# One chunk of the u products per head moved from the retrieval stage into the gate stage

## The chip, the cores and the metric

The kernel runs on one core of one Trainium2 chip. The metric is the device time of one execution in microseconds (us); lower is better. The engines are TensorE (PE for matmuls, PEld for its weight loads), VectorE (DVE), ScalarE (ACT), GpSimd (POOL) and SyncE (SP), which only issues transfers here.

## The reference, cut to what matters

The kernel computes one decoder layer: normalisation, attention and recurrence branches, their merge, and then a retrieval over 16384 single-neuron experts. Only this last part, `peer_ffn`, is touched. For 512 tokens it is

```python
q = (x_c @ w_q).reshape(128, 8, 256)              # 8 heads
s1, s2 = q[..., :128] @ sub_k1.T, q[..., 128:] @ sub_k2.T
t1, i1 = lax.top_k(s1, 16); t2, i2 = lax.top_k(s2, 16)
top_s, pos = lax.top_k(t1[..., :, None] + t2[..., None, :], 16)   # of the 256 sums
ids = the 16 of i1 * 128 + i2 at pos
gate = softmax(top_s)
hid = gelu(einsum('chkd,cd->chk', u[ids], x_c))
out = einsum('chk,chkd->cd', gate * hid, v[ids])
```

## The kernel before

The kernel does not gather u and v for most tokens. For three of the four tiles of 128 tokens (384 tokens) it computes the products of the tokens with **all** 16384 rows of u, in 128 chunks of 128 rows, applies gelu and stores 128 x 384 numbers per chunk in `HID_scratch`. It builds a matrix G of gates (expert by token, zero where an expert is not picked), multiplies the two and forms the product with all of v. The fourth tile's tokens gather their own rows of u and v instead, one gather of 128 rows (512 KB) per head and pick.

**A chunk m of the u products** (`hidden_layer`) is this chain: `load` brings 512 KB of u into a slot (L1377); `split_hi` on ScalarE rounds it to a high part (L1387); `split_lo` on VectorE makes the low part (L1397); `product` on TensorE is 8 x 3 matmuls of 384 columns (L88 to L90); `gelu` on ScalarE (L1393); `store` writes 192 KB to `HID_scratch` (L1381). There are five slots while the retrieval runs and two afterwards, so `load(m)` waits for `split_lo` of the chunk that had the slot before: five chunks back, later two chunks back.

**`peer_retrieval`** runs eight heads. Each head is a long chain of small steps on VectorE: the top 16 of 2 x 4 score tiles (L1580 to L1584), the candidate sums and their top 16 (L1607 to L1611), an index search (L1617 to L1640) that ends in the list of picks `gidx` (L1640), the softmax (L1650 to L1652). Between these steps stand, in an order written out by hand, 16 dot products of rows gathered for the previous head (`dot`, L1565) and the chunks' `split_lo` (`lo(h, j)` is that of chunk h * UPH + j + 2). TensorE does UPH chunks per head, and in the first seven heads the two projections and the scores of the next head (`project`, `score`). ScalarE and SP run matching loops. UPH is 13 before, so the retrieval does NRC = 8 * 13 + 2 = 106 chunks.

**`gate_matrix`** builds G in 96 steps of four tokens. VectorE makes one-hot rows (L1760, L1765), TensorE multiplies them (L1789), ScalarE copies the result into `g_stage` (L1803). Every 32 steps a tile is complete and SP stores its 8 MB as eight transfers of 1 MB (L1738). Beside the steps, each group of four steps takes one chunk: TensorE does a quarter of it per step, VectorE its `split_lo` after the fourth step, ScalarE `split_hi`, `gelu` and the store. BESIDE = 15 chunks are done so, up to chunk TAIL = 121; the other seven (121 to 127) follow behind the steps. GpSimd's queue is, in this order:

```python
for m in range(NRC + GSLOT, TAIL + GSLOT + 1):
    load(pool, m)                       # waits for split_lo of chunk m - 2
pool.wait_ge(g_stored[1], 8 * 16)       # tile 1 of G has been stored
for j in range(TOPK):                   # 16 gathers of the last head's rows, into g_stage's second half
    nc.gpsimd.indirect_dma_start(...)
for m in range(TAIL + GSLOT + 1, NCHUNK):
    load(pool, m)
```

VectorE, behind its last step, does `split_lo(TAIL + 1)`, waits until all 16 gathers have landed, and then does 16 dot products (L1774) with one `split_lo` ahead of every third, chunks 123 to 127. The stage ends when all engines are done and all stores have landed; then `experts` starts with the loads at L1861.

Of the kernel before, what the change touches and what calls it, by code (L numbers as in the profile page):

```python
# [35 lines left out]
NQ = SEQ // P  # L36
# [33 lines left out]
PH = 8  # L70
NK = 128
TOPK = 16
NCHUNK = 128
ND = 3
TD = ND * P
UPH = 13
USLOT = 5
GSLOT = 2
NRC = PH * UPH + 2
NCAND = 88  # L80
# [1338 lines left out]
def peer_retrieval(nc, d, keep):  # L1419
# [6 lines left out]
    with ExitStack() as ctx:  # L1426
# [46 lines left out]
        @block.sync  # L1473
        def _(sp):
            for m in range(PH * UPH):
                h, j = m // UPH, m % UPH
                if j in (0, 1) and h < PH - 1:
                    sp.wait_ge(w_lo, h * 2 + j + 1)
                    sp.dma_start(wraw[:, j], d["w_q"][h * 2 + j + 2]).then_inc(w_in[j], 16)
                if m >= 1:  # L1480
                    load(sp, m + USLOT - 1)
                    store(sp, m - 1)
            for m in range(PH * UPH - 1, NRC):
                store(sp, m)

        @block.scalar
        def _(act):
# [26 lines left out]
            for h in range(PH):  # L1514
                for j in range(UPH):
                    m = h * UPH + j
                    if h < PH - 1:
# [31 lines left out]
        def _(dve):  # L1549
# [7 lines left out]
            def dot(h, k):  # L1557

                if h == 0:
                    return  # L1560
                j = (h - 1) * TOPK + k
                dve.wait_ge(row_in[j % GBUF_R], j // GBUF_R * 16 + 16)
                if j > 0:
                    dve.wait_ge(rows_eaten, j)
                nc.vector.tensor_tensor_reduce(dump[:], urows[:, j % GBUF_R], x2t[:], 1.0, 0.0, ALU.mult, ALU.add,  # L1565
                                               hdot[:, j:j + 1]).then_inc(rows_eaten, 1)

            def lo(h, j):

                split_lo(dve, h * UPH + j + 2)  # L1570
# [5 lines left out]
            for h in range(PH):  # L1576
# [29 lines left out]
                for i in range(NQ):  # L1606
                    link(nc.vector.max(ctop[:, i, 0:8], cand[:, i]))  # L1607
                    link(nc.vector.match_replace(crest[:, i], ctop[:, i, 0:8], cand[:, i], -3.0e38))
                    nc.vector.max_index(cpos[:, i, 0:8], ctop[:, i, 0:8], cand[:, i])
                    link(nc.vector.max(ctop[:, i, 8:16], crest[:, i]))  # L1610
                    link(nc.vector.max_index(cpos[:, i, 8:16], ctop[:, i, 8:16], crest[:, i]))  # L1611
                    dot(h, 2 * NQ + i)
                    if h == PH - 1:
                        lo(h, 2 * NQ + i)
                    elif i != 1:
                        lo(h, (7, None, 8, 9)[i])
                nc.vector.tensor_tensor(shifted[:], ctop[:], ctop[:, :, 0:1].broadcast_to([P, NQ, TOPK]),  # L1617
# [13 lines left out]
                    eq[:].rearrange("p j q k a -> p (j q k) a"),  # L1631
                    cabf[:].rearrange("p j q k -> p (j q k)").unsqueeze(2).broadcast_to([P, 2 * NQ * TOPK, TOPK]),
                    iota[:].unsqueeze(1).broadcast_to([P, 2 * NQ * TOPK, TOPK]), ALU.is_equal))
                lo(h, 12 if h == PH - 1 else 10)
                flat = eq[:].rearrange("p j q k a -> p (j q) k a")
                link(nc.vector.tensor_tensor(
                    flat, flat, idxf[:].rearrange("p j q a -> p (j q) a").unsqueeze(2).broadcast_to([P, 2 * NQ, TOPK, TOPK]),
# [6 lines left out]
                    lo(h, 11)  # L1644
                for k in range(3 * NQ, TOPK):
                    dot(h, k)
                    if k == TOPK - 2 and h < PH - 1:
                        lo(h, 12)
                dve.wait_ge(exp_done, h + 1)
                link(nc.vector.reduce_sum(gsum[:, 0], gates[:], AX.X))  # L1650
                link(nc.vector.reciprocal(gsum[:, 1], gsum[:, 0]))
# [46 lines left out]
def gate_matrix(nc, d, keep):  # L1698
# [6 lines left out]
    TB = 4  # L1705
    NS = P // TB
    STEPS = ND * NS
    BESIDE = 15
    TAIL = NRC + BESIDE
    QA = NK // 8  # L1710
    NBANK = 4
    LATE = (PH - 1) * TOPK
    with ExitStack() as ctx:
# [18 lines left out]
        @block.sync  # L1732
        def _(sp):
            for tile in range(ND):
                sp.wait_ge(staged, NS * (tile + 1))
                for r in range(8):
                    a = slice(r * QA, (r + 1) * QA)
                    sp.dma_start(G[a, :, tile * P:tile * P + P].rearrange("a b t -> b a t"),  # L1738
                                 stage[:, tile % 2, a]).then_inc(g_stored[tile % 2], 16)
            sp.wait_ge(g_stored[0], 2 * 8 * 16)  # L1740
# [14 lines left out]
        def _(dve):  # L1755
            for n in range(STEPS):
# [6 lines left out]
                for t in range(TB):  # L1763
                    t1 = slice(n * TB + t, n * TB + t + 1)
                    nc.vector.tensor_scalar(hot1[:, b, t], iota[:], picksT[:, 0, t1], picksT[:, 2, t1],  # L1765
                                            ALU.is_equal, ALU.mult).then_inc(hot1_made, 1)
                if n % 4 == 3 and n // 4 <= BESIDE:
                    split_lo(dve, NRC + n // 4)
# [10 lines left out]
        def _(pe):  # L1779
            for n in range(STEPS):  # L1780
                if 4 <= n < 4 + 4 * BESIDE:
                    i = n % 4
# [11 lines left out]
        @block.scalar  # L1794
        def _(act):
            for n in range(STEPS):
                tile, i = n // NS, n % NS
                if n % 4 == 0 and n // 4 <= BESIDE:
                    split_hi(act, NRC + n // 4)
                if tile >= 2 and i == 0:  # L1800
                    act.wait_ge(g_stored[tile % 2], 8 * 16 * (tile // 2))
                act.wait_ge(placed, n + 1)
                nc.scalar.copy(stage[:, tile % 2, :, i * TB:i * TB + TB].rearrange("p a t -> p t a"),  # L1803
                               ps[:, n % NBANK]).then_inc(staged, 1)
                if n % 4 == 1 and 2 <= n // 4 <= BESIDE + 1:
                    gelu(act, NRC + n // 4 - 2)
                    store(act, NRC + n // 4 - 2)
            for m in range(TAIL, NCHUNK):
                if m + 1 < NCHUNK:
                    split_hi(act, m + 1)  # L1810
                gelu(act, m)
                store(act, m)
            all_stored(act)
# [141 lines left out]
def build(nc, d):  # L1955

    with ExitStack() as ctx:
# [49 lines left out]
        with ExitStack() as mid:  # L2007
            keep["picksT"] = mid.enter_context(nc.sbuf_tensor("picksT", [P, 3, TD], F32))
            for name in ("x2h", "x2l"):
                keep[name] = mid.enter_context(nc.sbuf_tensor(name, [P, KD, SEQ], F32R))  # L2010
            keep["h_ps"] = mid.enter_context(nc.psum_tensor("h_ps", [P, 2, 512], F32))
            keep["hid"] = mid.enter_context(nc.sbuf_tensor("h_hid", [P, 2, TD], F32))
            keep["iota128"] = mid.enter_context(nc.sbuf_tensor("g_iota128", [P, NK], F32))
            keep["tables_in"] = mid.enter_context(nc.semaphore("tables_in"))
            for name, dt in (("uraw", F32), ("uh", F32R), ("ul", F32R)):
                lower = mid.enter_context(nc.sbuf_tensor("h_" + name, [P, GSLOT, KD, P], dt))
                keep[name] = [lower[:, i] for i in range(GSLOT)]
            queries = mid.enter_context(ExitStack())
            upper = queries.enter_context(nc.sbuf_tensor("hu_uraw", [P, USLOT - GSLOT, KD, P], F32))
            keep["uraw"] = keep["uraw"] + [upper[:, i] for i in range(USLOT - GSLOT)]  # L2020
            keep["h_sem"] = lambda name: mid.enter_context(nc.semaphore("h_" + name))
            keep["u_in"] = [keep["h_sem"](f"u_arrived{b}") for b in range(USLOT)]
            for name, shape in (("subk", [P, 2, NK]), ("iota16", [P, TOPK])):
                keep[name] = queries.enter_context(nc.sbuf_tensor("q_" + name, shape, F32))
            keep["q_wraw"] = queries.enter_context(nc.sbuf_tensor("q_wraw", [P, 2, KD, P], F32))
            keep["q_w_in"] = [mid.enter_context(nc.semaphore(f"q_w_arrived{b}")) for b in range(2)]
            second_norm(nc, d, keep)
            early.close()
            peer_retrieval(nc, d, keep)
            queries.close()  # L2030
            gate_matrix(nc, d, keep)
# [78 lines left out]
```

## Time and profile before

| | us |
|---|---|
| median of 3 runs | 2096.08 |
| lowest and highest | 2094.06 and 2100.32 |
| the profiled execution | 2095.05 |
| its span, first to last instruction | 2093.2 |
| mean granted TensorE clock | 0.971 |

| engine | busy us | share of the span |
|---|---|---|
| PE | 1933.1 | 92% |
| PEld | 1660.6 | 79% |
| DVE | 1454.6 | 69% |
| ACT | 767.1 | 37% |
| POOL | 336.9 | 16% |

In the profiled execution the retrieval runs from about 785 to 1326 us, the gate steps from 1330 to 1508, the chunks behind them to 1546, and `experts` from 1553.8 to the end. A line of the timeline gives an instruction's start, its duration, engine, source line, operation and tiles; in square brackets stand the engine's idle time before it and what ended it. Instructions of VectorE overlap their neighbours a little, and matmuls are pipelined, so what one costs in a row of them is read from start to start. A line such as `A <- B: 9.4, 1, 9.4` of the waits says that A waited for B 9.4 us in total, once, at most 9.4 us.

### The profile page before, as it was taken

Reading aid. Unit: us, or ns where it says so; the run is one execution under the profiler, and the core shown is the slowest. Engines: PE = TensorE matmul, PEld = TensorE weight load, DVE = VectorE, ACT = ScalarE, POOL = GpSimd, SP = SyncE. Lnnn points to the kernel's source line nnn. Section 1 sums busy time; section 2 is a strip of 40 time slices with the busy share of each in tenths; the row PEclk is TensorE's granted clock in tenths of the full one; section 3 lists DMA queues with packets and bytes.
Section 4 is the critical chain, followed back from the end, with each engine's and each line's share of the span. In section 5 each row is a group of like instructions: output and inputs, shape, how many; then the busy total and the mean of one; then the engine's idle time right before and its main releaser. Section 6 shows DMA issues by size and latency. Waiting matters only on the chain. (4 is left out here: it accounts for less than half of the span.)

```text
span 2093.2 us, 34968 instructions
## 1 busy us (share of the span) xinstructions
PE 1933.1 (92%) x13881; PEld 1660.6 (79%) x13881; DVE 1454.6 (69%) x3024; ACT 767.1 (37%) x1177; POOL 336.9 (16%) x317
## 2 busy tenths in 40 slices
PE   7999998888885959999999999899769999999999
PEld 6998666666662439999999999899657888888887
DVE  4253434454544136899999999899858888888887
ACT  5332335212213023433343433477523333333332
POOL 1001100000000000322233313000314222322221
PEclk9999999999997989999999999899979999999999
DMA  3222101100003043866887668157999999999997
GB/s 134 87 82 80 41 21 61 51 3 3 3 3 161 0 155 111 314 249 244 299 327 275 243 255 331 60 164 217 286 328 398 357 356 358 348 368 355 354 353 269
DMA packets 191906, 424.01 MB, mean 203 GB/s; under 512 B 16896, under 2 KB 116480, under 8 KB 190720
## 3 DMA queue, kind: packets, MB, share of 16 engines
q1 hardware_dynamic: 148832, 272.74, 37.8%
q0 software_dynamic: 39744, 144.72, 18.4%
q10 hardware_dynamic: 3168, 4.33, 0.6%
q8 instruction: 110, 1.80, 0.4%
q14 instruction: 52, 0.43, 0.1%
HBM read 367.16 MB, written 54.53 MB: 201 GB/s over the span
## 5 line engine op out<-in xcount | busy, mean ns | idle before, releaser
L88 PE MATMUL eo_ps<-vh,e_wh 128*128 128x512 f32 x768 | 300.4, 391 | 17.6 <-DVE e_wl L1931 17.5
L89 PE MATMUL eo_ps<-vh,e_wl 128*128 128x512 f32 x768 | 299.8, 390 | 0.0
L90 PE MATMUL eo_ps<-vl,e_wh 128*128 128x512 f32 x768 | 299.7, 390 | 0.0
L1544 POOL DMA_INDIRECT q_urows<-in_u_rows,gidx x112 | 136.5, 1219 | 872.8 <-DVE gidx L1640 718.1
L1881 ACT CAST vh<-vraw 128x1024 fp32r<-128x1024 f32 x128 | 135.0, 1055 | 321.7 <-PE eo_ps L90 303.4
L1922 DVE TENSOR_TENSOR vl<-vraw,vh 128x1024 fp32r<-128x1024 f32 x128 | 156.7, 1224 | 81.9 <-ACT vh L1881 81.7
L1898 POOL DMA_INDIRECT e_rows<-in_v,gidx x128 | 141.7, 1107 | 388.0 <-DVE e_acc_t L1912 348.1
L88 PE MATMUL h_ps<-x2h,h_uh 128*128 128x384 f32 x520 | 180.4, 347 | 6.6 <-DVE h_ul L1397 6.6
L88 PEld LDWEIGHTS eo_ps<-vh,e_wh 128*128 128x128 f32 x768 | 144.9, 189 | 49.2 <-DVE vl L1922 15.1
L90 PE MATMUL h_ps<-x2l,h_uh 128*128 128x384 f32 x520 | 174.8, 336 | 0.0
L89 PE MATMUL h_ps<-x2h,h_ul 128*128 128x384 f32 x520 | 174.7, 336 | 0.0
L1393 ACT ACTIVATE h_hid<-h_ps 128x384 f32<-128x384 f32 x128 | 63.5, 496 | 290.5 <-PE h_ps L90 209.8
L88 PE MATMUL h_ps<-x2h,q_uh 128*128 128x384 f32 x504 | 169.7, 337 | 0.0
L90 PE MATMUL h_ps<-x2l,q_uh 128*128 128x384 f32 x504 | 169.5, 336 | 0.0
L89 PE MATMUL h_ps<-x2h,q_ul 128*128 128x384 f32 x504 | 169.4, 336 | 0.0
L90 PEld LDWEIGHTS eo_ps<-vl,e_wh 128*128 128x128 f32 x768 | 144.8, 189 | 30.3
L89 PEld LDWEIGHTS eo_ps<-vh,e_wl 128*128 128x128 f32 x768 | 144.9, 189 | 29.9
L1912 DVE SCALAR_TENSOR_TENSOR e_acc_t<-e_rows,e_w_t,e_acc_t 128x1024 f32<-128x1024 f32 x128 | 163.8, 1279 | 3.7 <-DMA e_rows<-in_v,gidx 3.5
L1565 DVE CUSTOM_DVE_ANT_0 q_dump<-q_urows,x2t 128x1024 f32<-128x1024 f32 x112 | 137.4, 1227 | 5.2
L88 PE MATMUL ps_z<-xh,wh 128*128 128x264 f32 x432 | 125.8, 291 | 6.0 <-DVE xl L347 6.0
L1789 PE MATMUL g_ps<-g_hot 128*128 128x128 f32 x768 | 107.1, 284 | 19.0 <-DVE g_hot L1765 18.9
L1803 ACT COPY g_stage<-g_ps 128x512 f32<-128x512 f32 x96 | 103.3, 1078 | 57.0 <-PE g_ps L1789 57.0
(301 smaller groups left out, 4208.1 us busy)
## 6 DMA issues: line engine op xcount, KB each, us to landing
vraw<-in_v SPq DMA_DIRECT2D x128, 512.0 KB, 7.3
hu_uraw<-in_u SPq DMA_DIRECT2D x63, 512.0 KB, 7.2
G_scratch<-g_stage SPq DMA_DIRECT2D x24, 1024.0 KB, 11.6
gm<-G_scratch SPq DMA_DIRECT2D x128, 192.0 KB, 5.9
e_hid<-HID_scratch SPq DMA_DIRECT2D x128, 192.0 KB, 7.6
h_uraw<-in_u SPq DMA_DIRECT2D x45, 512.0 KB, 6.9
wraw<-in_w_z SPq DMA_DIRECT2D x43, 512.0 KB, 3.5
HID_scratch<-h_hid SPq DMA_DIRECT2D x106, 192.0 KB, 4.1
```

The costliest lines, as they stand in the source:

```text
L88: nc.tensor.matmul(out, a[0], b[0], start=start, stop=False)
L89: nc.tensor.matmul(out, a[1], b[0], start=False, stop=False)
L90: return nc.tensor.matmul(out, a[0], b[1], start=False, stop=stop)
L1393: nc.scalar.activation(hid[:, m % 2], h_ps[:, m % 2, 0:TD], ACT.Gelu).then_inc(hid_out, 1)
L1544: nc.gpsimd.indirect_dma_start(urows[:, j % GBUF_R], None, d["u_rows"], bass.IndirectOffsetOnAxis(ap=gidx[:, j:j + 1], axis=0)).then_inc(r ...
L1565: nc.vector.tensor_tensor_reduce(dump[:], urows[:, j % GBUF_R], x2t[:], 1.0, 0.0, ALU.mult, ALU.add, hdot[:, j:j + 1]).then_inc(rows_eaten, 1)
L1789: mm = nc.tensor.matmul(ps[:, n % NBANK, j], hot2[:, n % 2, j], hot1[:, n % 2, j], start=True, stop=True)
L1803: nc.scalar.copy(stage[:, tile % 2, :, i * TB:i * TB + TB].rearrange("p a t -> p t a"), ps[:, n % NBANK]).then_inc(staged, 1)
L1881: nc.scalar.copy(vh[:, c % WSLOT], vraw[:, c % VSLOT]).then_inc(v_hi, 1)
L1898: nc.gpsimd.indirect_dma_start(rows[:, j % GBUF_E], None, d["v"].rearrange("c p n -> (c p) n"), bass.IndirectOffsetOnAxis(ap=gidx[:, j:j + ...
L1912: nc.vector.scalar_tensor_tensor(out=acc_t[:], in0=rows[:, j % GBUF_E], scalar=w_t[:, j:j + 1], in1=acc_t[:], op0=ALU.mult, op1=ALU.add).t ...
L1922: nc.vector.tensor_tensor(vl[:, b], vraw[:, s], vh[:, b].bitcast(F32), ALU.subtract).then_inc(v_lo, 1)
```

## The change

Each head of the retrieval does 12 chunks in place of 13, so NRC is 98, and 23 chunks in place of 15 run beside the gate steps: TAIL stays 121. The `split_lo` that stood between the last two dot products of the first seven heads is gone, and in the last head the one behind the fourth candidate tile. ScalarE's exponential of the softmax moves with the last chunk of a head from j = 12 to j = 11, where the copy of the next head's scores also stands. With 23 chunks beside 24 groups of steps, the gelu and store of chunk 120 no longer fit in the loop of the steps: BEHIND = 120 makes the loop behind them begin one chunk earlier. The loads of the moved chunks go from SP's queue to GpSimd's, their stores from SP's to ScalarE's.

```diff
-UPH = 13
+UPH = 12
@@ peer_retrieval, VectorE
                     if h == PH - 1:
-                        lo(h, 2 * NQ + i)
+                        if i < NQ - 1:
+                            lo(h, 2 * NQ + i)
...
-                lo(h, 12 if h == PH - 1 else 10)
+                lo(h, 11 if h == PH - 1 else 10)
...
                 for k in range(3 * NQ, TOPK):
                     dot(h, k)
-                    if k == TOPK - 2 and h < PH - 1:
-                        lo(h, 12)
@@ gate_matrix
-    BESIDE = 15
+    BESIDE = 23
+    BEHIND = NRC + min(BESIDE + 1, STEPS // 4 - 1) - 1
     TAIL = NRC + BESIDE
@@ gate_matrix, ScalarE
-            for m in range(TAIL, NCHUNK):
-                if m + 1 < NCHUNK:
+            for m in range(BEHIND, NCHUNK):
+                if TAIL < m + 1 < NCHUNK:
                     split_hi(act, m + 1)
                 gelu(act, m)
                 store(act, m)
```

## Rows read from the trace of the kernel before

**Rows 1.** Busy time of each engine in one head's stretch (us, instructions, clock, DMA).

```profile
1052.00:1119.10 67.10, 67.10 (x378) 64.90 (x377) 64.27 (x164) 25.60 (x36) 19.64 (x16) 1.00 0.77 282
```

**Rows 2.** VectorE's waits: stretch 783 to 850, then 1051 to 1119.

```profile
DVE q_ul L1397 <- ACT q_uh L1387: 8.6, 4, 5.7
...
DVE q_ul L1397 <- ACT q_uh L1387: 0.3, 1, 0.3
```

**Rows 3.** Timeline of TensorE inside a chunk of the retrieval.

```profile
1060.06 0.34 PE L88 MATMUL h_ps<-x2h,q_uh 128*128 128x384 f32 x1
...
1060.58 0.34 PE L88 MATMUL h_ps<-x2h,q_uh 128*128 128x384 f32 x1
```

**Rows 4.** Timeline of VectorE around the split that the change removes.

```profile
1054.59 1.23 DVE L1565 CUSTOM_DVE_ANT_0 q_dump<-q_urows,x2t 128x1024 f32<-128x1024 f32 x1
...
1055.97 1.22 DVE L1565 CUSTOM_DVE_ANT_0 q_dump<-q_urows,x2t 128x1024 f32<-128x1024 f32 x1
...
1057.12 1.22 DVE L1397 TENSOR_TENSOR q_ul<-hu_uraw,q_uh 128x1024 fp32r<-128x1024 f32 x1
1058.26 1.22 DVE L1565 CUSTOM_DVE_ANT_0 q_dump<-q_urows,x2t 128x1024 f32<-128x1024 f32 x1
```

**Rows 5.** Timeline of TensorE: two gate steps that have a chunk beside them.

```profile
1400.30 1.05 PE L1789 MATMUL g_ps<-g_hot 128*128 128x128 f32 x8
...
1402.23 1.05 PE L1789 MATMUL g_ps<-g_hot 128*128 128x128 f32 x8
```

**Rows 6.** TensorE's waits: stretch 1332 to 1456, then 1456 to 1562.

```profile
PE g_ps L1789 <- DVE g_hot L1765: 3.7, 2, 3.4
...
PE g_ps L1789 <- DVE g_hot L1765: 15.3, 32, 0.7
```

**Rows 7.** Timeline of TensorE: gate steps 63 and 95 (the last).

```profile
1454.43 1.05 PE L1789 MATMUL g_ps<-g_hot 128*128 128x128 f32 x8
...
1506.64 1.16 PE L1789 MATMUL g_ps<-g_hot 128*128 128x128 f32 x8 [0.47 <-DVE g_hot L1765]
```

**Rows 8.** Timeline of GpSimd: load of chunk 122, first and last gather, load of 124.

```profile
1447.07 0.53 POOL L1377 DMA_DIRECT2D h_uraw<-in_u  x1 [7.21 <-DVE h_ul L1397]
...
1489.15 1.14 POOL L1748 DMA_INDIRECT g_stage<-in_u_rows,gidx  x1 [33.82 <-DMA G_scratch<-g_stage]
...
1512.13 0.94 POOL L1748 DMA_INDIRECT g_stage<-in_u_rows,gidx  x1 [0.30 <-issue]
1513.07 0.58 POOL L1377 DMA_DIRECT2D h_uraw<-in_u  x1
```

**Rows 9.** Timeline of VectorE: the splits of chunks 122 and 123.

```profile
1509.80 1.23 DVE L1397 TENSOR_TENSOR h_ul<-h_uraw,h_uh 128x1024 fp32r<-128x1024 f32 x1 [3.21 <-ACT h_uh L1387]
1520.44 1.22 DVE L1397 TENSOR_TENSOR h_ul<-h_uraw,h_uh 128x1024 fp32r<-128x1024 f32 x1 [9.42 <-DMA g_stage<-in_u_rows,gidx]
```

**Rows 10.** Landings by tile: gathers 1 and 2, 14 to 16, load 124.

```profile
DMA to landing us min/median/max: 4.5/5.0/5.5
...
DMA to landing us min/median/max: 7.6/8.2/8.3
...
DMA to landing us min/median/max: 9.2/9.2/9.2
```

**Rows 11.** Landings by tile: tile 2's first two G stores; HID_scratch's last store.

```profile
DMA to landing us min/median/max: 14.8/16.8/18.8
...
DMA to landing us min/median/max: 5.2/5.2/5.2
```

**Rows 12.** Busy time, clock, DMA share, GB/s while tile 2's G stores run.

```profile
1508.90:1553.40 44.50, 30.34 (x162) 29.37 (x160) 25.49 (x38) 9.56 (x14) 5.45 (x8) 0.88 1.04 334
```

**Rows 13.** Timelines: ScalarE's last store in the stage, SP's first load behind it.

```profile
1546.37 0.33 ACTq L1381 DMA_DIRECT2D HID_scratch<-h_hid  x1
...
1553.78 0.34 SPq L1861 DMA_DIRECT2D vraw<-in_v  x1
```

**Rows 14.** Timeline of TensorE: first matmul of chunk 123.

```profile
1521.72 0.69 PE L88 MATMUL h_ps<-x2h,h_uh 128*128 128x384 f32 x1 [5.57 <-DVE h_ul L1397]
```

## The prediction

> **What bounds the kernel now.** I read the views in this order: the busy shares of the page, the span cut into windows by stage and by head, the waits of each engine in these windows, and then timelines where a wait ended. The page alone misleads. It shows TensorE at 92% of the span and VectorE at 69%, which suggests that only TensorE's work counts. The windows say something else about the stages that the change touches.
>
> In the heads of the retrieval (a window from one head's list of picks to the next), TensorE is busy for all 67.1 us, but VectorE for 64.3 us of them [rows 1], and it waits only 0.3 us in a head [rows 2]. The other 2.5 us are the gaps between dependent instructions: two dots that follow each other start 1.38 us apart, though a dot that is followed by a split takes 1.15 us [rows 4]. So two chains of nearly the same length run beside each other. TensorE's is 67.1 us, VectorE's about 66.9.
>
> In the gate steps that have a chunk beside them, TensorE sets the pace: steps are 1.93 us apart [rows 5], and it hardly waits (3.7 us in all) [rows 6]. In the 32 steps without a chunk it waits for VectorE's one-hot rows at each step, 15.3 us in 32 waits [rows 6], and a step takes (1506.64 - 1454.43) / 32 = 1.63 us [rows 7].
>
> Behind the steps neither engine is the bound. VectorE stands 9.4 us for the gathers of the last head's rows [rows 9], TensorE 5.6 us behind it [rows 14], and the stage ends when the last stores have landed: `experts` starts at 1553.78 [rows 13].
>
> **The change, part by part.** Times are on the clock of the profiled execution.
>
> (a) Retrieval, one chunk less per head. Three matmuls take 0.52 us from start to start [rows 3], so a chunk's 24 take 4.16 us, and a head would be 62.9 us of TensorE. VectorE loses far less: a split holds it for 1.14 us [rows 4], and since the two dots around it now follow each other, 1.38 - 1.15 = 0.23 us of gap comes back. That leaves 0.91 us, and with the wait of 0.25 us gone [rows 2] a head shortens by 1.16 us. After that VectorE is the bound, and TensorE idles some 3 us per head. The first interval is different: head 0 has no dots and VectorE waits for TensorE there (8.6 us in four waits) [rows 2], so it takes TensorE's 4.16. Sum from list to list: 4.2 + 5 x 1.16 + (0.91 + 1.14) for the last, which loses two splits, = 12.0 us. Bounds: 9 (the first interval saves no more than the others, since the first rows then come late for head 1's dots) to 12.5.
>
> (b) Gate steps, eight more chunks. 32 steps go from 1.63 to 1.93 us: 61.9 in place of 52.2, +9.7 us. The start of the last step moves from 1506.64 to 1516.3. This is close to certain, since 60 steps of this form are in the trace. ScalarE's moved `split_hi`, `gelu` and store, and the loads on GpSimd's queue, already ran in this form in the first groups and nobody waited for them; they cost nothing there.
>
> (c) Behind the steps: GpSimd's queue. Before, the last `load` in the steps (chunk 123) waited for the split of 121 at step 63, and GpSimd then stood for tile 1's stores and began the 16 gathers at 1489.15, 17 us before the last step [rows 8]. Now the split of 121 comes at step 95. All gathers, and the loads of 124 to 127 behind them, move behind the last gate step. Let Q be the end of the last step's matmuls (1507.8 before). The load of chunk 122 shows the lag: step 59 began 24 steps of 1.93 us behind 1400.30 [rows 5], so its matmuls ended at 1447.7, and the load, released by the split of that step, was issued 0.7 us before that, at 1447.07 [rows 8]. It takes 0.5 us, so the first gather can be issued at about Q + 0.2. A gather without company lands 4.5 us after its issue [rows 10]. But these meet tile 2's G stores, which start at Q + 1.1. In the trace the last three gathers and the load behind them met the same stores: the third last gather, issued two gaps of 1.24 us before 1512.13, landed 7.6 us later at 1517.3; the last landed after 8.3 us at 1520.4; the load issued at 1513.07 after 9.2 at 1522.3 [rows 8, 10]. That is 1.6 to 1.9 us apart. With 1.8 us each for 15 more gathers and for the load ahead of them, all rows are in at Q + 0.2 + 4.5 + 16 x 1.8 = Q + 33.5. Before it was 1520.44 - 1507.8 = Q + 12.6 [rows 9]. All that hangs on it (splits of 123 to 127, 16 dots, five chunks, the last store) keeps its order: from 1520.44 to the last HID store's landing at 1546.37 + 5.2 = 1551.6 [rows 11, 13] it is 31.1 us. With 0.4 us to the next stage, `experts` starts at Q + 65.0, before at Q + 46.0 [rows 13]: +19.0 us.
>
> I hold the bytes against it. From 1508.9 to 1553.4 the engines moved 334 GB/s at a full DMA share [rows 12]: 8.4 MB of G, six gathers, four loads and the HID stores, 15 MB. Now 16 gathers and five loads fall into it, 21 MB: 62 us. The chain of 65 and the bytes agree.
>
> Lower bound: only the issue counts, 1.24 us per gather (0.94 + 0.30) [rows 8], with the last landing 8.3 us later: Q + 27.1, +12.6. Upper bound: below, in the second rival.
>
> (d) The gelu of chunk 120 moved behind the loop and ScalarE's exponential moved to j = 11: the first lies in a stretch where TensorE has 8 us of products in hand and then waits for the gathers; the second waits for a result that VectorE has ready before the ninth product ends. I cost both at nothing; if the second is late, it delays `split_hi` of the chunk after next, which has 1.3 us of slack.
>
> **Sum**: -12.0 + 9.7 + 19.0 = +16.7 us, so 2095.05 + 16.7 = 2111.8. The profiled execution lies 1.0 us under the median of the runs; on the median it is 2112.8.
>
> **The rivals.**
>
> *The heads follow TensorE (not slower).* Page and windows show TensorE at 100% in the heads. If VectorE's 2.5 us of gaps shrink when it is pressed, each head saves 4.16 us, 33.3 in all: 2096.1 - 33.3 + 28.7 = 2091.5. The sign turns where a head saves over 28.7 / 8 = 3.6 us. Against it: the gaps stand between dependent instructions and repeat to 0.01 us, and only 0.3 us per head is a wait for somebody.
>
> *The gathers and the G stores share evenly.* The first G store took 14.8 us to land against the gathers' 7.6 to 8.3 [rows 10, 11], so in the trace the stores gave way. If both got half of 334 GB/s, 16 gathers and a load (8.9 MB) would take 53 us; G would be stored by then, and what follows is VectorE's 16 dots and five splits, 21 x 1.15 = 24 us, and some 3 for the last chunk's end. That is Q + 80, +34, and 2128. The Trainium skill (DMA: Bandwidth & Descriptors, section "Queues, rings and completion order") says that each DMA engine takes turns between its queues, a packet at a time. By that rule GpSimd's queue would get no more than its turn, and the time would be this rival's; the landings above speak against equal bytes, not against turns.
>
> *TensorE's clock falls in the heads.* TensorE would idle some 3 us in each head. In the trace it idled 5.6 us, the next matmuls took 0.52 to 0.69 us where 0.33 is usual, and the granted clock of that stretch averages under full speed [rows 12, 14]. A head has 3 us of room for that. If the clock fell for long enough to add 5 us, six heads would lose 2 us each: +12, 2125. [...] No row shows an idle time of 3 us followed by such work, so it stays open.
>
> *GpSimd's late start is hidden*, because the G stores end the stage anyway. Then only (a) and (b) count: 2096.1 - 12.0 + 9.7 = 2093.8. Against it: 6 MB more have to pass in the same stretch, at a DMA share of 1 [rows 12].
>
> **How the numbers follow.** Forecast 0.70; TensorE's heads 0.05; even sharing 0.11; clock 0.08; hidden start 0.06. The forecast's own range is 2105 (lower bound of (c)) to 2117 (the heads save 9, the landings 1.9 us apart). The range reaches up to even sharing and the clock, and somewhat under the lower bound: 2101 to 2127. A measurement of this kernel can tell about 0.3% (6.3 us) from no change, so "same" is 2089.8 to 2102.4: the first and last rivals and a low end of the forecast, 0.09. Faster needs both the heads of the first rival and a short tail: 0.03. Slower: 0.88.
>
> **What would show it.** In the profile after: heads 66 us apart with VectorE without waits and TensorE waiting about 3 us for a split per head; gate steps 1.93 us apart to the end; first gather issued behind the last gate step; VectorE's wait for the gathers near 28 us in place of 9.4 and TensorE's near 25 in place of 5.6; tile 2's first G stores landing later than 15 us. What would make it wrong: gathers that land far from 1.8 us apart beside the G stores, or heads of 63 us.

## The result and the profile after

| | before | after |
|---|---|---|
| median of 5 runs, us | 2096.08 | 2109.78 |
| lowest and highest | 2094.06 and 2100.74 | 2109.21 and 2112.73 |
| profiled execution | 2095.05 | 2109.21 |
| its span | 2093.2 | 2107.4 |

The change makes the kernel slower: the ratio of after to before is 1.0063, with a 95% interval of 1.0046 to 1.0079. That is 13.7 us on the medians; the prediction had 16.7.

Three stretches of the two traces add up to the difference of the spans. Q is again the end of the last gate step's matmuls.

| stretch, us | before | after | difference |
|---|---|---|---|
| start of the span to the start of the last step of head 7's softmax | 1326.08 | 1316.92 | -9.2 |
| from there to Q | 181.7 | 190.6 | +8.9 |
| Q to the first load of `experts` | 46.0 | 60.6 | +14.6 |
| `experts` | 539.5 | 539.3 | -0.2 |

**The heads.** The timeline of VectorE after the change shows five lists of picks, 65.9, 66.4 and 66.0 us apart in the last three intervals, and where head 7 ends (columns as in the timelines above: start, duration, engine, line, operation):

```profile
850.50 0.17 DVE L1641 SCALAR_TENSOR_TENSOR gidx<-q_picks 128x16 uint32<-128x16 f32 x1
...
915.69 0.18 DVE L1641 SCALAR_TENSOR_TENSOR gidx<-q_picks 128x16 uint32<-128x16 f32 x1
...
981.58 0.17 DVE L1641 SCALAR_TENSOR_TENSOR gidx<-q_picks 128x16 uint32<-128x16 f32 x1
...
1048.00 0.17 DVE L1641 SCALAR_TENSOR_TENSOR gidx<-q_picks 128x16 uint32<-128x16 f32 x1
...
1114.00 0.18 DVE L1641 SCALAR_TENSOR_TENSOR gidx<-q_picks 128x16 uint32<-128x16 f32 x1
...
1316.92 0.22 DVE L1651 TENSOR_TENSOR q_picks<-q_gates,q_gsum 128x64 f32<-128x64 f32 x1
```

The windows of two heads answer to [rows 1]. TensorE is no longer busy throughout, VectorE still is for all but its gaps:

```profile
981.60:1048.00 66.40, 63.77 (x348) 61.24 (x347) 63.25 (x163) 24.02 (x33) 18.72 (x16) 0.97 0.75 271
1048.00:1114.00 66.00, 64.40 (x360) 61.87 (x359) 63.16 (x164) 24.01 (x33) 18.73 (x16) 1.00 0.77 280
```

**The gate steps.** TensorE's last two steps are 1.93 us apart, which answers to [rows 5, 7]: the last steps now have the pace of the first.

```profile
1504.53 1.05 PE L1789 MATMUL g_ps<-g_hot 128*128 128x128 f32 x8
1506.46 1.05 PE L1789 MATMUL g_ps<-g_hot 128*128 128x128 f32 x8
```

**Behind the steps.** GpSimd's timeline answers to [rows 8]: the load of chunk 123, the first and the last gather, and the load of 124. The first gather is issued 18.5 us later than before, 0.2 us behind Q = 1507.5.

```profile
1506.83 0.53 POOL L1377 DMA_DIRECT2D h_uraw<-in_u  x1 [7.21 <-DVE h_ul L1397]
1507.67 0.99 POOL L1748 DMA_INDIRECT g_stage<-in_u_rows,gidx  x1 [0.30 <-issue]
...
1526.53 0.94 POOL L1748 DMA_INDIRECT g_stage<-in_u_rows,gidx  x1 [0.30 <-issue]
1527.47 0.58 POOL L1377 DMA_DIRECT2D h_uraw<-in_u  x1
```

VectorE waits for them 26.45 us where [rows 9] show 9.42, TensorE behind it 23.24 us where [rows 14] show 5.57, and SP starts `experts` 60.6 us behind Q:

```profile
1538.20 1.23 DVE L1397 TENSOR_TENSOR h_ul<-h_uraw,h_uh 128x1024 fp32r<-128x1024 f32 x1 [26.45 <-DMA g_stage<-in_u_rows,gidx]
```

```profile
1539.48 0.69 PE L88 MATMUL h_ps<-x2h,h_uh 128*128 128x384 f32 x1 [23.24 <-DVE h_ul L1397]
```

```profile
1568.13 0.34 SPq L1861 DMA_DIRECT2D vraw<-in_v  x1
```

### The profile page after: what moved, and what is told of

The parts are those of the page before. It is cut to its first block and busy times, and to the rows that moved or that the text cites. A ratio compares the mean times of both kernels' runs of the same rounds, so it can differ in the third digit from the quotient of the medians.

```text
span 2107.4 us, 34968 instructions
## 1 busy us (share of the span) xinstructions
PE 1932.3 (92%) x13881; PEld 1663.0 (79%) x13881; DVE 1455.3 (69%) x3024; ACT 764.1 (36%) x1177; POOL 331.0 (16%) x325
## 5 line engine op out<-in xcount | busy, mean ns | idle before, releaser
L1544 POOL DMA_INDIRECT q_urows<-in_u_rows,gidx x112 | 130.5, 1165 | 870.4 <-DVE gidx L1641 715.8
L88 PE MATMUL h_ps<-x2h,h_uh 128*128 128x384 f32 x560 | 197.7, 353 | 35.3 <-DVE h_ul L1397 29.9
L90 PE MATMUL h_ps<-x2l,h_uh 128*128 128x384 f32 x560 | 188.9, 337 | 0.0
L89 PE MATMUL h_ps<-x2h,h_ul 128*128 128x384 f32 x560 | 188.8, 337 | 0.0
L89 PEld LDWEIGHTS eo_ps<-vh,e_wl 128*128 128x128 f32 x768 | 144.9, 189 | 29.9
L88 PE MATMUL h_ps<-x2h,q_uh 128*128 128x384 f32 x464 | 157.9, 340 | 8.0 <-issue 6.3
L90 PE MATMUL h_ps<-x2l,q_uh 128*128 128x384 f32 x464 | 157.4, 339 | 0.0
L89 PE MATMUL h_ps<-x2h,q_ul 128*128 128x384 f32 x464 | 157.3, 339 | 0.0
L88 PEld LDWEIGHTS h_ps<-x2h,h_uh 128*128 128x128 f32 x560 | 106.6, 190 | 37.8 <-DVE h_ul L1397 31.6
## 6 DMA issues: line engine op xcount, KB each, us to landing
G_scratch<-g_stage SPq DMA_DIRECT2D x24, 1024.0 KB, 12.6
```

Source lines behind the costliest of these rows:

```text
L88: nc.tensor.matmul(out, a[0], b[0], start=start, stop=False)
L89: nc.tensor.matmul(out, a[1], b[0], start=False, stop=False)
L90: return nc.tensor.matmul(out, a[0], b[1], start=False, stop=stop)
L1544: nc.gpsimd.indirect_dma_start(urows[:, j % GBUF_R], None, d["u_rows"], bass.IndirectOffsetOnAxis(ap=gidx[:, j:j + 1], axis=0)).then_inc(r ...
```

## The experiments

The theory under test has two halves. First, the loss behind the steps is GpSimd's queue: the 16 gathers stand behind a load that now waits for the last steps. Second, with 12 chunks VectorE sets the pace of the heads, with 13 TensorE does.

### Free the queue: e1_loads_on_act

```diff
 GpSimd
-for m in range(NRC + GSLOT, TAIL + GSLOT + 1):
-    load(pool, m)
 pool.wait_ge(g_stored[1], 8 * 16)
... (semaphores of their own for the loads of 124 to 127)
 ScalarE, in the loop of the gate steps
+if n % 4 == 0 and 1 <= n // 4 <= BESIDE:
+    load(act, NRC + n // 4 + 1)
 and behind it
+load(act, TAIL + GSLOT)
```

> The kernel after, with one thing changed: the loads of chunks 100 to 123 are issued on ScalarE's queue between the gate steps, so that GpSimd's queue holds only the wait for tile 1's G stores, the 16 gathers and the loads of 124 to 127. Heads and gate steps keep their 23 chunks. Theory (the 16 gathers stand behind the load of chunk 123 on GpSimd's queue): the first gather is issued near 1487 us, when tile 1 is stored, about 20 us before the last gate step ends; VectorE waits 5 to 10 us for them in place of 26.5, the next stage starts about 46 us behind the last gate step in place of 60.6, and the time falls by 13 to 15 us, to 2095 to 2097. Rival (the bytes of the G stores end this stage and the late gathers hide behind them): the time stays within 3 us of 2110.

Measured: median 2097.2 us, ratio to before 1.0003 (0.9993 to 1.0012). Of the 13.7 us, 12.6 are gone, and no difference from the kernel before can be told. The first line is from the timeline of GpSimd, then come the waits of VectorE behind the steps, then SP's first load of `experts` (last gate step's end: 1506.8):

```profile
1485.31 0.97 POOL L1747 DMA_INDIRECT g_stage<-in_u_rows,gidx  x1 [199.11 <-DMA G_scratch<-g_stage]
```

```profile
DVE h_ul L1398 <- DMA g_stage<-in_u_rows,gidx: 10.4, 1, 10.4
```

```profile
1554.97 0.34 SPq L1863 DMA_DIRECT2D vraw<-in_v  x1
```

The gathers start when tile 1 is stored, 21.5 us ahead of Q, VectorE waits 10.4 us (5 to 10 expected), and `experts` starts at Q + 48.2. The heads and the steps are those of the kernel after (65.2, 65.9, 66.4 us; 185.4 us of steps against 185.5). The rival, that the late gathers hide behind the stores' bytes, falls: the same bytes pass here. Behind the steps 2.2 us of the loss are left (Q + 48.2 against Q + 46.0 before). They are the rows again: the last gather lands at Q + 14.6 here and at Q + 12.6 before.

### Only the late gathers: e2_late_gathers

```diff
 pool.wait_ge(g_stored[1], 8 * 16)
+pool.wait_ge(hot1_made, STEPS * TB)
```

> The kernel before (13 chunks per head, 15 beside the steps), with one wait added: GpSimd begins the 16 gathers only when VectorE has made the last one-hot rows. Nothing else differs. Theory (late gathers are the whole loss behind the steps): first gather at about 1507 us in place of 1489, all rows in near Q + 30 (Q: end of the last gate step, 1507.8), the next stage at Q + 60 in place of Q + 46, time 2096 + 14 = 2110, so the same time as the kernel after. Rival (the gathers cost nothing, the loss is elsewhere, for instance in the denser gate steps): within 3 us of 2096.

Measured: median 2109.8 us, ratio 1.0059 (1.0042 to 1.0077), the time of the kernel after. Its waits of VectorE behind the steps:

```profile
DVE h_ul L1397 <- DMA g_stage<-in_u_rows,gidx: 27.1, 1, 27.1
```

`experts` starts at 1569.21, Q + 61.3. So the kernel before, with nothing changed but the time at which the gathers may start, loses what the kernel after loses. The two runs bracket the cause from both sides.

### Less work for VectorE: e3_after_short_dots and e4_before_short_dots

```diff
-nc.vector.tensor_tensor_reduce(dump[:], urows[:, j % GBUF_R], x2t[:], ...)
+w = 64 if k in (2, 14) else D
+nc.vector.tensor_tensor_reduce(dump[:, 0:w], urows[:, j % GBUF_R, 0:w], x2t[:, 0:w], ...)
```

> The kernel after, with two of the 16 dot products per head (k = 2 and 14) cut from 1024 to 64 columns, so that part of the fourth tile's u products is left out. This takes about 1.0 us of VectorE from each, 2 us per head. Theory (VectorE sets the pace of the heads after the change): heads shrink from 66.1 to about 64.1 us, still above TensorE's 62.9, and the time falls by some 12 to 14 us. Rival (the heads follow TensorE): the heads stay at 66 and the time within 3 us.

> The kernel before, with the same two dot products per head cut to 64 columns (part of the fourth tile's u products is left out). Theory (with 13 chunks TensorE sets the pace, VectorE has only 0.25 us of waits): heads stay at 67.0 us or above 66.8, VectorE's waits grow by 2 us per head, and the time falls by at most 4 us (2 of them in the last head, which has no projections). Rival (VectorE sets the pace of the heads in both kernels): heads of 65.1 us, 12 to 14 us less.

Measured, in one execution each: 2091.4 us on the kernel after, 2093.3 on the kernel before. The lists of picks show it head by head. With 12 chunks:

```profile
977.12 0.18 DVE L1642 SCALAR_TENSOR_TENSOR gidx<-q_picks 128x16 uint32<-128x16 f32 x1
...
1040.98 0.17 DVE L1642 SCALAR_TENSOR_TENSOR gidx<-q_picks 128x16 uint32<-128x16 f32 x1
```

With 13 chunks:

```profile
987.38 0.18 DVE L1641 SCALAR_TENSOR_TENSOR gidx<-q_picks 128x16 uint32<-128x16 f32 x1
...
1054.54 0.17 DVE L1641 SCALAR_TENSOR_TENSOR gidx<-q_picks 128x16 uint32<-128x16 f32 x1
```

Taking 2 us of work from VectorE shortens a middle head with 12 chunks from 65.9 or more to 63.9 or 64.0, and one with 13 chunks not at all: 67.16. This is the second half of the theory, and the rival that the heads follow TensorE after the change falls. The 18 us that e3 gained on the kernel after are more than the 12 to 14 expected; 16.5 of them are in the retrieval (its last step at 1300.4 against 1316.9), where the first interval lost 1.2 and the others 1.9 to 2.6 each.

### The first interval: e5_first_rows

```diff
-for j in range((PH - 1) * TOPK):          # GpSimd's gathers
+for j in range(4, (PH - 1) * TOPK):
...
-nc.vector.tensor_tensor_reduce(dump[:], urows[:, j % GBUF_R], x2t[:], ...)
+nc.vector.tensor_tensor_reduce(dump[:], urows[:, j % GBUF_R] if j >= 4 else x2t[:], x2t[:], ...)
```

> The kernel after, without the first four gathers of head 0's rows: the four dot products that would read them read x2t instead (four products of the fourth tile are left out). In the kernel after, VectorE stands 4.7 us at the first of these dots and the first interval between two lists is 65.2 us, where the prediction had 62.9. Theory (these rows come late, since VectorE reaches the dot 3 us earlier than before): the wait of 4.7 us is gone, the first interval is 62.5 to 63.5 us, the time is 1 to 3 us below the kernel after (2109.8). Rival (the first interval is bound by something else, such as TensorE's chunks or the splits of ScalarE): it stays at 65.2 us.

In the kernel after, VectorE stands 4.65 us ahead of head 1's first dot. The view names no releaser there (`issue`), since no landing of these rows is in this trace; in e1, which has the same heads, the same wait of 4.7 us is put down to the gathered rows:

```profile
858.77 1.23 DVE L1565 CUSTOM_DVE_ANT_0 q_dump<-q_urows,x2t 128x1024 f32<-128x1024 f32 x1 [4.65 <-issue]
```

Without the first four gathers the wait is gone and the two first lists are 62.9 us apart:

```profile
855.66 0.17 DVE L1642 SCALAR_TENSOR_TENSOR gidx<-q_picks 128x16 uint32<-128x16 f32 x1
...
918.55 0.17 DVE L1642 SCALAR_TENSOR_TENSOR gidx<-q_picks 128x16 uint32<-128x16 f32 x1
```

So the interval is bound by the rows' arrival in the kernel after, and by TensorE without it (TensorE is busy for all 62.9 us). The wait has two sources. VectorE is ready for the dot 3.6 us behind the list of picks in place of 6.6. And the rows come later too: the first gather of head 0, issued 0.5 us behind the list in both kernels, takes 2.0 us longer to land with 12 chunks. From its landings, in the kernel before and in e1:

```profile
DMA to landing us min/median/max: 5.7/5.7/5.7
...
DMA to landing us min/median/max: 7.7/7.7/7.7
```

Rows that came as early as before would have left a wait of some 2.5 us in place of 4.65, and by that estimate an interval near 63 us; so most of the 2.3 us over 62.9 is the later landing. With 12 chunks SP issues one transfer more just ahead of it, the next projection's weights 1.9 us before the list; whether this delays the rows was not tested. The time of this one execution, 2114.9 us, does not show the gain: this execution reached the first list 5.2 us later, at 855.7, in a part that the edit does not touch, and was 1.9 us slower behind the steps.

### TensorE's clock in the heads: e6_fill

```diff
 for j in range(UPH):
+    if h > 0 and j == 2:
+        for _ in range(8):
+            nc.tensor.matmul(fill[:, 0:TD], x2h[:, 0, 0:P], x2h[:, 0, 0:TD], start=True, stop=True)
     product(pe, h * UPH + j)
```

> The kernel after, with eight matmuls of 384 columns added in heads 1 to 7 ahead of the third chunk, where TensorE waits 2.6 us for a split; their result is not used. They take about 1.4 us of this wait. In the kernel after the granted clock fell to half behind two of these waits, and the intervals of 66.4 us in place of 65.9 are those two. Theory (the fall of the clock costs 0.5 us in such a head): no fall in the heads, all five middle intervals 65.9 us, the retrieval about 1 us shorter. Rival (the 66.4 us have another cause, such as late loads): two or more intervals stay at 66.4 us.

TensorE's timeline in the kernel after, in the interval of 66.4 us. It waits 2.63 us, and 0.8 us later the matmuls are 0.32 us apart in place of 0.17, until 997.2. The last line is a window over this stretch: the granted clock is 0.50, the lower of its two levels (1.2 in place of 2.4 GHz), for 3.4 us.

```profile
992.98 0.44 PE L88 MATMUL h_ps<-x2h,q_uh 128*128 128x384 f32 x1 [2.63 <-issue]
...
994.46 0.52 PE L88 MATMUL h_ps<-x2h,q_uh 128*128 128x384 f32 x1
994.78 0.52 PE L89 MATMUL h_ps<-x2h,q_ul 128*128 128x384 f32 x1
...
997.25 0.34 PE L88 MATMUL h_ps<-x2h,q_uh 128*128 128x384 f32 x1
```

```profile
993.70:997.10 3.40, 3.40 (x13) 3.40 (x12) 3.33 (x8) 0.00 (x0) 1.52 (x3) 0.50 1.04 415
```

This happened in two of the five middle intervals, and these are the two of 66.4 us. Four of the heads have such a wait of 2.6 to 2.7 us, and behind two of them the clock stayed up. Behind each fall the next head's wait is 1.6 us, and no wait of 1.6 us is followed by one. Other traces with the same heads bear this out: in e1 and e7 one of the two falls lies in another head, and again the intervals of 66.4 us are those with a fall and no others. With the filling matmuls the wait is 1.21 us and the matmuls behind it keep their pace:

```profile
992.98 0.44 PE L88 MATMUL h_ps<-x2h,q_uh 128*128 128x384 f32 x1 [1.21 <-DVE q_ul L1397]
993.27 0.34 PE L89 MATMUL h_ps<-x2h,q_ul 128*128 128x384 f32 x1
...
995.00 0.34 PE L90 MATMUL h_ps<-x2l,q_uh 128*128 128x384 f32 x1
```

All five middle intervals are 65.9 to 66.0 us, and the retrieval ends at 1315.8 in place of 1316.9. The theory holds: the clock costs 0.5 us in each head in which it falls.

### Fewer chunks beside the steps: e7_beside20

On top of e1_loads_on_act:

```diff
-BESIDE = 23
+BESIDE = 20
-split_lo(dve, TAIL + 1)
+for m in range(1, 4):
+    split_lo(dve, TAIL + m)
 dve.wait_ge(rows_in, TOPK * 16)
... (the later splits, the loads and their semaphores shifted to match)
```

> The kernel with the loads on ScalarE's queue, with 20 chunks beside the gate steps in place of 23: ten chunks behind the steps, three splits ahead of VectorE's wait for the gathers in place of one. Theory (a chunk beside the steps costs 1.2 us, and behind them TensorE has room, since it works 31 of the 48 us there): gate steps 3.6 us shorter, the stage behind them 48 to 50 us, time 2094 to 2096. Rival (the stage behind the steps is bound by TensorE's chunks as well as by the stores): it grows by the 12.5 us of three chunks less the waits, to 55 us, and the time is 2099 to 2103.

Measured: 2099.8 us, ratio to before 1.0011 (1.0000 to 1.0021). My theory was wrong. The rival has the numbers right, but not the reason. The steps got 3.3 us shorter (182.1 against 185.4), but `experts` starts at Q + 54.3 in place of Q + 48.2. VectorE's splits behind the steps wait for ScalarE, which waits for the loads of u (17.2 us in seven waits):

```profile
1506.31 1.22 DVE L1398 TENSOR_TENSOR h_ul<-h_uraw,h_uh 128x1024 fp32r<-128x1024 f32 x1 [3.21 <-ACT h_uh L1388]
1510.55 1.23 DVE L1398 TENSOR_TENSOR h_ul<-h_uraw,h_uh 128x1024 fp32r<-128x1024 f32 x1 [3.01 <-ACT h_uh L1388]
1516.09 1.23 DVE L1398 TENSOR_TENSOR h_ul<-h_uraw,h_uh 128x1024 fp32r<-128x1024 f32 x1 [4.32 <-ACT h_uh L1388]
1521.82 1.23 DVE L1398 TENSOR_TENSOR h_ul<-h_uraw,h_uh 128x1024 fp32r<-128x1024 f32 x1 [4.50 <-ACT h_uh L1388]
```

With two slots, a load can start only after the split two chunks back, and beside the G stores GpSimd's loads take 6.3 to 9.4 us to land, where one alone took 3.7 in the kernel before. The four splits above are 5.2 us apart on average, more than TensorE's 4.2 for a chunk. So the chain of load and splits sets the pace there, not TensorE, and TensorE's idle time was no room for more chunks.

### Another engine for two splits: e8_pool_split

On top of e1_loads_on_act:

```diff
 VectorE
-if h < PH - 1 and (b, i) in ((0, 3), (1, 1)):
-    split_w(h + 1, b)
 GpSimd, between the gathers
+if j // TOPK + 2 < PH and j % TOPK in (9, 11):
+    split_w(j // TOPK + 2, j % TOPK // 11)
... (head 1's two splits stand ahead of the first gather)
```

> The kernel with the loads on ScalarE's queue, and the two splits per head of the next head's projection weights moved from VectorE to GpSimd, which puts them between its gathers. VectorE loses 2.3 us per head. Theory (VectorE sets the pace of the heads with 12 chunks and TensorE has 3 us of room): heads go from 66.1 to about 63.9 us as they did with two short dots, the time falls by 13 to 15 us to 2082 to 2084. Rivals: GpSimd is slower at this split than VectorE, or slows it down, or its gathers come late behind it; then VectorE waits for rows and the heads stay at 65 us or more.

Measured: 2116.6 us, ratio 1.0090 (1.0068 to 1.0111). The theory was wrong, and the rival that GpSimd slows VectorE down came true: heads grew to 68.4 to 69.1 us although VectorE had lost two splits. GpSimd takes 2.41 us for a split, and the dots of VectorE that ran into its two splits in a head took 3.96 and 2.71 us in place of 1.23:

```profile
1143.65 2.41 POOL L1543 TENSOR_TENSOR q_wl<-q_wraw,q_wh 128x1024 fp32r<-128x1024 f32 x1
...
1153.12 2.40 POOL L1543 TENSOR_TENSOR q_wl<-q_wraw,q_wh 128x1024 fp32r<-128x1024 f32 x1
```

```profile
1143.19 3.96 DVE L1574 CUSTOM_DVE_ANT_0 q_dump<-q_urows,x2t 128x1024 f32<-128x1024 f32 x1
...
1153.90 2.71 DVE L1574 CUSTOM_DVE_ANT_0 q_dump<-q_urows,x2t 128x1024 f32<-128x1024 f32 x1
```

In one head the 16 dots together, with what follows each, took 5.5 us more than in e1. A dot was not slowed a little: both ended 1.1 us behind the end of GpSimd's instruction, nearly the length of a whole dot. The small steps with one input in SBUF (`MAX8`, 0.28 us) kept their length beside it.

The Trainium skill (SBUF — State Buffer, section "SBUF: two separate sides") says that a VectorE instruction with two inputs in SBUF and a GpSimd instruction that reads SBUF exclude each other for a whole instruction. The trace agrees: each dot got through only when GpSimd's instruction was over. It also says that the one that starts first goes first. The first pair of records does not show this: the dot's begins 0.46 us earlier and ends last.

### A shorter step on VectorE: e9_bf16_picks and e10_bf16_before

```diff
-idxf = sb("idxf", [P, 2, NQ, TOPK])
+idxf = sb("idxf", [P, 2, NQ, TOPK], BF16)
-cabf = sb("cabf", [P, 2, NQ, TOPK])
-eq = sb("eq", [P, 2, NQ, TOPK, TOPK])
+cabf = sb("cabf", [P, 2, NQ, TOPK], BF16)
+eq = sb("eq", [P, 2, NQ, TOPK, TOPK], BF16)
+iotab = sb("iotab", [P, TOPK], BF16)      # a copy of iota, used in the comparison
...
```

> The kernel with 12 chunks per head and the loads on ScalarE's queue (e1_loads_on_act), with VectorE's two index-search steps over 2048 elements (the comparison, 2.29 us, and the multiplication, 2.28 us) and their operands in bfloat16 in place of float32; all values are whole numbers up to 127, so nothing is rounded. Theory (VectorE sets the pace of the heads, and TensorE has 3 us of room): each microsecond that these steps lose is a microsecond of each head, until TensorE's 62.9. If one of them halves, heads of 64.8 us and a time near 2089; if both do, 63.6 us and near 2081; if none does, 65.9 and 2097. Rival (the heads do not follow VectorE): the steps get shorter but the heads stay at 66 us.

> The kernel before (13 chunks per head) with the same change of the two steps to bfloat16. Theory (TensorE sets the pace with 13 chunks): heads stay at 67.15 us whatever the steps lose, VectorE only waits longer; the last head and the way to its end get shorter by what the steps lose, so the time falls by 0 to 4 us. Rival (VectorE sets the pace in both kernels): heads shorter by 1 to 2 us and a time of 2082 to 2089.

Measured: with 12 chunks 2089.2 us, ratio to before 0.9972 (0.9960 to 0.9985); with 13 chunks 2097.5 us, ratio 1.0012 (1.0000 to 1.0023). One of the two steps halved, the multiplication; the comparison kept its 2.29 us. From the trace with 12 chunks:

```profile
1039.23 1.22 DVE L1641 TENSOR_TENSOR q_eq<-q_eq,q_idxf 128x2048 bf16<-128x2048 bf16 x1
```

The middle heads are 64.8 to 65.0 us apart with 12 chunks, 1.0 to 1.1 less than in e1 where its clock stays up, and the step lost 1.06: the case that was forecast for one step. TensorE's waits are 1.2 us there where they were 2.6, and the granted clock is 1.00 in all these heads, as e6 would have it. With 13 chunks the heads did not get shorter. They even grew, to 67.6 to 67.9 us. No single matmul waits there; many matmuls of a chunk start 0.175 to 0.182 us apart in place of 0.173, in both kernels with bfloat16. The reason stays open.

## Why the prediction was right

The forecast held in sign and in mechanism, and the size was near: +13.7 us for +16.7. Some of that nearness is luck. The heads saved 2.8 us less than forecast and the stretch behind the steps lost 4.4 us less, and these two misses partly cancel. The four steps, by their own terms:

**(a) The heads: -12.0 predicted, -9.2 measured** (-9.1 from list to list, which is what the sum counts). The idea was right: e3 against e4 and e9 against e10 show that the binding engine changes from TensorE to VectorE. The middle intervals are 65.9 to 66.0 us where the clock stays up; the prediction's 67.15 - 1.16 = 66.0. The last is 64.75, predicted 66.77 - 2.05 = 64.7. The mis-sized term is the first interval: 65.2 us in place of 62.9. That TensorE bound it before is right, and VectorE waited 5.1 us in it. But the 8.6 us of [rows 2] that the prediction quoted for it lie ahead of the first list, and they are waits for ScalarE's high parts. With 12 chunks VectorE came to head 1's first dot before the rows did and stood 4.65 us. The prediction named this as its bound of 9 and then did not take it; e5 shows that the wait for these rows is the cause. What no term had is that the rows themselves land 2.0 us later than before. The clock took another 2 x 0.5 us.

**(b) The gate steps: +9.7 predicted, +9.6 measured** (185.5 us against 175.9 from the first matmul to Q; 32 x 1.93 is 61.8, so the sum itself gives 9.6). The way from the last head to the steps was 0.7 us shorter, which I had not in the sum. It takes 4.8 to 5.8 us in the other traces with either number of chunks, so it is not shown to belong to the change; why it varies is open.

**(c) Behind the steps: +19.0 predicted, +14.6 measured.** The place, the cause and the order are right, and shown by e1 and e2. The size was off in two terms. The rows were in at Q + 30.7, not Q + 33.5: from the 4.5 us after the first issue, the 16 transfers took 26 us, 1.6 us each in place of 1.8. The windows show why the estimate from the bytes leaned the same wrong way. In this stretch more passed per second than the 334 GB/s of [rows 12], most of all while the gathers ran (the last number of a line is GB/s):

```profile
1508.60:1568.10 59.50, 30.61 (x162) 29.33 (x160) 25.50 (x38) 10.01 (x15) 16.49 (x20) 0.79 1.02 351
1518.00:1538.00 20.00, 0.00 (x0) 0.00 (x0) 0.00 (x0) 0.20 (x1) 7.91 (x9) 0.53 1.04 409
```

And from the rows' arrival to `experts` it took 29.9 us in place of 31.5: the last chunk's store was issued at 1564.56, and `experts` began 3.6 us later where the prediction carried over a landing of 5.2 and 0.4. The 5.2 us were measured beside the G stores, which now are done by then; in e2, where this landing is on record, it took 1.9 us.

**(d) The moved gelu and exponential: nothing, as predicted.** VectorE waits for ScalarE only 0.9 us in all heads together in the kernel after, and never for the exponential. Behind the steps, e2 has late gathers and no moved gelu, and takes 30.9 us from the rows' arrival to `experts`; the kernel after, which has the moved gelu, takes 29.9. One wait that the prediction did not name appeared in the last head: TensorE stood 3.7 us for a gelu of ScalarE. It delayed no list, since the last interval is the 64.7 us that were forecast for VectorE.

**The rivals.** Heads that follow TensorE: ruled out by e3. Even sharing of the transfers, at Q + 80: ruled out. Most bytes went to the gathers again. The two queues from 1512 to 1538, first GpSimd's, then SP's with the G stores (packets, MB, share of the 16 engines' time):

```profile
q0 software_dynamic: 2269, 8.28, 78.1%
q1 hardware_dynamic: 3169, 1.61, 20.6%
```

By packets the two are of one order, by bytes they are five to one, since GpSimd's packets are of 4 KB and the stores' of 512 bytes. So turns between queues, as the Trainium skill has them (DMA: Bandwidth & Descriptors, section "Queues, rings and completion order"), need not be even shares of the bytes; what a turn is cannot be read from these records. A hidden start: ruled out by e1 and e2. The falling clock was half right: it does fall behind waits of 2.6 us, in two of the five middle intervals, but for 3.4 us at the lower level each, which eats into TensorE's spare time and leaves 0.5 us, not 2.

## What to carry to other kernels

When work moves beside another stage, follow every queue that it joins to its end: here eight loads cost nothing by themselves, but the last of them waited for the last step, and 16 gathers stood behind it in the same queue. Two engines that were busy 96% and 100% of a stage were both at the limit here; removing 4.16 us from one gave 1.2 us, because the other took over, and the way to tell them apart is to shorten the same instruction in both versions, as e3 and e4 do for VectorE. The measured version that pays is the one that does all three things: 12 chunks per head, the loads on a queue with nothing behind them, and a shorter step on the engine that now binds (e9, 0.28% faster than before).

## What the runs showed of the hardware

- An elementwise instruction on GpSimd (2.41 us, both inputs in SBUF) held up a dot on VectorE until it was over: 3.96 and 2.71 us in place of 1.23 (e8). Issuing gathers from GpSimd beside the same dots did not (1.23 us each).
- A multiplication of 2048 elements per partition took 2.28 us in float32 and 1.22 in bfloat16, but a comparison of the same size with one operand repeated along the inner dimension took 2.29 us in both (e9, e10).
- Of four waits of TensorE of 2.6 to 2.7 us in the heads of the kernel after, two were followed by 3.4 us at half the clock; of the waits of 1.2 us in e6, none.
- Gathers of 512 KB beside 1 MB stores in packets of 512 bytes landed 1.75 us apart on average in e2 (26.3 us for 15), the last of them 1.5 us apart. Before tile 2's stores began, the ten of the kernel before landed 1.76 us apart, issued 1.6 us apart. So the gathers lost nothing, and the stores gave way: the second of them took 29 us to land in e2 and 19 in the kernel before.
